# Shifting where TensorE's activations begin in SBUF, and keeping each row of 1/rms once

## The reference

```python
h = rms(x);  p = h @ w_in                        # 1024 -> 5120: q,k,v of two branches, two gates
y_a = moba(p) @ w_br_moba                        # 8 heads of 64; one block of 256: causal softmax + ALiBi
y_b = stick_breaking(p) @ w_br_sb                # 8 heads of 64; sigmoid(z) * exp(-later softplus sums)
x = x + (sigmoid(gate_a) * y_a + sigmoid(gate_b) * y_b) @ w_out
m = rms(mem)                                     # 256 memory tokens
x = x + cross_attention(rms(x) @ w_xq, m @ w_xkv) @ w_xo      # 4 heads of 128
x = x + square(relu(rms(x) @ w_up)) @ w_down     # 1024 -> 4096 -> 1024
return rms(x)
```

## Time and profile before

| | |
|---|---|
| median of 3 runs | 427.58 us |
| the profiled execution | 427.64 us, of which the span from first to last instruction is 425.5 us |
| TensorE (PE) | 413.5 us busy, 97%, 2839 matmuls |
| weight loads (PEld) | 381.0 us, 90% |
| VectorE (DVE) | 336.2 us, 79% |
| ScalarE (ACT) | 251.0 us, 59% |
| GpSimd (POOL) | 25.4 us, 6% |
| DMA | 77.47 MB, mean 182 GB/s |
| granted TensorE clock, mean | 0.995 of full speed |

### The profile page before, as it was taken

The page is one execution under the profiler, slowest core; times in us unless marked ns, Lnnn a source line. Parts: engine busy times, 40 slices in busy tenths (PEclk is TensorE's granted clock), DMA queues, the critical chain, the costliest instruction groups (busy, mean ns, idle before and its releaser), DMA issues.

```text
span 425.5 us, 7066 instructions
## 1 busy us (share of the span) xinstructions
PE 413.5 (97%) x2839; PEld 381.0 (90%) x2839; DVE 336.2 (79%) x448; ACT 251.0 (59%) x300; POOL 25.4 (6%) x39
## 2 busy tenths in 40 slices
PE   8999999999999999999999999999999999999992
PEld 7999988999999999889998899899999999999971
DVE  5588556967757536874856899999999999999956
ACT  7663238763665534551556468767777777776523
POOL 0069000000000000000200000000000000000002
PEclk9999999999999999999999999999999999999997
DMA  8999554434335255554443245465556555564002
GB/s 274 420 418 379 192 197 166 157 124 150 100 104 193 100 197 194 175 188 172 164 175 123 102 169 189 152 216 199 203 200 201 199 205 199 203 203 181 2 0 99
DMA packets 12539, 77.47 MB, mean 182 GB/s; under 512 B 1376, under 2 KB 1376, under 8 KB 4064
## 3 DMA queue, kind: packets, MB, share of 16 engines
q1 hardware_dynamic: 12512, 77.09, 50.0%
HBM read 76.04 MB, written 1.05 MB: 181 GB/s over the span
## 4 chain that ended last, share of the span: by engine, by line
PE 84%; DVE 6%; ACT 5%; issue 2%; DMA 1%; POOL 0%; POOLq 0%; SPq 0%; DVEq 0%; ACTq 0%
PE bank L1088 39%; PE bank L1354 15%; PE bank L1107 13%; PE bank L1202 10%; PE bank L1214 1%; ACT w_hi L415 1%; DVE res L1019 1%; DMA head_all<-in_head_dram 1%; DVE w_lo L662 1%; PE bank L1300 1%; DVE t_lo L662 1%; PE bank L1320 1%; DVE t_sum L914 1%; ACT mT_hi L427 1%; DVE f_lo L662 1%
## 5 line engine op out<-in xcount | busy, mean ns | idle before, releaser
L662 DVE TENSOR_TENSOR w_lo<-raw,w_hi 128x2048 fp32r<-128x2048 f32 (+2 forms) x87 | 147.4, 1702 | 26.5 <-ACT w_hi L415 25.5
L1088 PE MATMUL bank<-hT_hi,w_hi 128*128 128x256 f32 x416 | 118.4, 285 | 1.3 <-DVE w_lo L662 0.7
L1088 PE MATMUL bank<-hT_lo,w_hi 128*128 128x256 f32 x416 | 117.7, 283 | 0.0
L1088 PE MATMUL bank<-hT_hi,w_lo 128*128 128x256 f32 x416 | 117.7, 283 | 0.0
L1088 PEld LDWEIGHTS bank<-hT_hi,w_hi 128*128 128x128 f32 x416 | 79.7, 192 | 2.7 <-DVE hT_lo L712 1.1
L1088 PEld LDWEIGHTS bank<-hT_lo,w_hi 128*128 128x128 f32 x416 | 79.7, 192 | 0.6
L1088 PEld LDWEIGHTS bank<-hT_hi,w_lo 128*128 128x128 f32 x416 | 79.7, 192 | 0.0
L415 ACT ACTIVATE w_hi<-raw 128x2048 fp32r<-128x2048 f32 x33 | 62.8, 1913 | 28.2 <-PE bank L1088 15.0
L1202 PE MATMUL bank<-hT_hi,w_hi 128*128 128x256 f32 x128 | 37.1, 290 | 0.1
L662 DVE TENSOR_TENSOR t_lo<-t_sum,t_hi 128x1024 fp32r<-128x1024 f32 x30 | 36.4, 1212 | 0.0
L1202 PE MATMUL bank<-hT_lo,w_hi 128*128 128x256 f32 x128 | 36.2, 283 | 0.0
(11 more groups left out here) (195 smaller groups left out, 817.9 us busy)
## 6 DMA issues: line engine op xcount, KB each, us to landing
raw<-in_weights_dram SPq DMA_DIRECT2D x65, 1024.0 KB, 4.8
head_all<-in_head_dram SPq DMA_DIRECT2D x7, 256.0 KB, 4.8
raw<-in_chunk_dram SPq DMA_DIRECT2D x4, 256.0 KB, 5.8
raw<-in_chunk_dram SPq DMA_DIRECT2D x2, 512.0 KB, 6.9
res<-in_x_dram SPq DMA_DIRECT2D x2, 512.0 KB, 10.8
mem_tok<-in_mem_dram SPq DMA_DIRECT2D x1, 1024.0 KB, 11.5
memT_raw<-in_memT_dram SPq DMA_DIRECT2D x1, 1024.0 KB, 10.2
out_dram<-xs SPq DMA_DIRECT2D x2, 512.0 KB, 2.7
```

Of the source, the lines that this page charges most:

```text
L662: return nc.vector.tensor_tensor(dst, whole, high.bitcast(fp32), sub)
L1088: last = mm(outs[m], w, v[:, k0 + k, :], start=first and n == 0, stop=k == nk - 1 and n == 2, skip_group_check=bool(kt_wait))
```

## The change

1. `hT_hi`, `mT_hi` and `aT_hi` begin 192 bytes past a multiple of 512, `hT_lo`, `mT_lo` and `aT_lo` 320 bytes; the weights stay at 128. The high part so begins 64 bytes and the low part 192 bytes from the weights' place. `t_hi`, `f_hi`, `f_lo` and everything after them stay at 128.
2. `rstd_row` and `mem_row` hold their 256 values once; `spread` makes one copy instead of two, and the evacuations read the row twice through a broadcast pattern of [128, 2, 256]. The copies of `aT` in cross-attention take a two-block form too, since `aT` is now a slice.

```diff
+        def skip_to(place_in_512):
+            at[0] += (place_in_512 - at[0]) % 512
+        def by_tokens(name, step, place_in_512):
+            skip_to(place_in_512)
+            return place(name, [P, KT, SEQ + step // 4], f32r)
...
-        hT_hi = sb("hT_hi", [P, KT, SEQ], f32r)
-        hT_lo = sb("hT_lo", [P, KT, SEQ], f32r)
+        hT_hi_all, _ = by_tokens("hT_hi", 0, 192)
+        hT_hi = hT_hi_all[:, :, 0:SEQ]
+        hT_lo_all, _ = by_tokens("hT_lo", 0, 320)
+        hT_lo = hT_lo_all[:, :, 0:SEQ]
+        skip_to(128)
...     (mT_hi, mT_lo, aT_hi, aT_lo alike)
-        rstd_row = sb("rstd_row", [P, 2, SEQ])
-        mem_row = sb("mem_row", [P, 2, SEQ])
+        rstd_row = sb("rstd_row", [P, SEQ])
+        mem_row = sb("mem_row", [P, SEQ])
...
-                for j in range(2):
-                    last = nc.vector.tensor_copy(dst[:, j, :], bank[b][:, 0:SEQ])
-                last.then_inc(row_ready, 1)
+                nc.vector.tensor_copy(dst[:, :], bank[b][:, 0:SEQ]).then_inc(row_ready, 1)
...
-                nc.vector.tensor_tensor(flat(gateT[:, 2 * h:2 * h + 2, :]), bank[h % 2][:, :],
-                                        flat(rstd_row[:, :, :]), ALU.mult).then_inc(gate_evac, 1)
+                nc.vector.tensor_tensor(gateT[:, 2 * h:2 * h + 2, :], halves_of(bank[h % 2][:, :]),
+                                        twice(rstd_row[:, :]), ALU.mult).then_inc(gate_evac, 1)
```

More of the change, by code:

```diff
@@ L143, in hybrid_layer @@
         res = sb("res", [P, TOK, D])
-        hT_hi = sb("hT_hi", [P, KT, SEQ], f32r)
-        hT_lo = sb("hT_lo", [P, KT, SEQ], f32r)
-        mT_hi, o = place("mT_hi", [P, KT, SEQ], f32r)
+        hT_hi_all, _ = by_tokens("hT_hi", 0, 192)
[3 more added lines that the diff above has]
+        skip_to(128)
+        o = at[0]
+        mT_hi_all, _ = by_tokens("mT_hi", 0, 192)
+        mT_hi = mT_hi_all[:, :, 0:SEQ]
+        mT_lo_all, _ = by_tokens("mT_lo", 0, 320)
+        mT_lo = mT_lo_all[:, :, 0:SEQ]
+        skip_to(128)
         t_hi = sb("t_hi", [P, 2, 4 * 512], f32r, over=o)
-        mT_lo = sb("mT_lo", [P, KT, SEQ], f32r)
         qkT, o = place("qkT", [P, 16, SEQ])
@@ L166, in hybrid_layer @@
         mem_tok = sb("mem_tok", [P, TOK, D], over=o + 8192)
-        aT_hi, o = place("aT_hi", [P, 8, SEQ], f32r)
+        o = at[0]
+        aT_hi_all, _ = by_tokens("aT_hi", 0, 192)
+        aT_hi = aT_hi_all[:, :, 0:SEQ]
+        aT_lo_all, _ = by_tokens("aT_lo", 0, 320)
+        aT_lo = aT_lo_all[:, :, 0:SEQ]
+        skip_to(128)
         f_hi = sb("f_hi", [P, 2, 8 * P], f32r, over=o)
-        aT_lo, o = place("aT_lo", [P, 8, SEQ], f32r)
-        f_lo = sb("f_lo", [P, 2, 8 * P], f32r, over=o)
+        f_lo = sb("f_lo", [P, 2, 8 * P], f32r, over=o + 8192)
         alibi, o = place("alibi", [P, HEADS, SEQ])
@@ L549, in _ @@
                 act.wait_ge(x_av, 2 * p + 2)
-                copy(flat(aT_hi[:, 2 * p:2 * p + 2, :]), bank[p][:, :], ACT.Copy).then_inc(xo_hi, 1)
+                copy(aT_hi[:, 2 * p:2 * p + 2, :], bank[p].rearrange("p (b q) -> p b q", b=2), ACT.Copy)\
+                    .then_inc(xo_hi, 1)
             def arrived(c, i):
@@ L703, in spread, with halves_of, twice @@
                 dve.wait_ge(row_done, rows)
-                for j in range(2):
-                    last = nc.vector.tensor_copy(dst[:, j, :], bank[b][:, 0:SEQ])
-                last.then_inc(row_ready, 1)
+                nc.vector.tensor_copy(dst[:, :], bank[b][:, 0:SEQ]).then_inc(row_ready, 1)
+            def halves_of(t):
+                return t.rearrange("p (a n) -> p a n", a=2)
+            def twice(row):
+                return row.rearrange("p (a n) -> p a n", a=1).to_broadcast([P, 2, SEQ])
             nc.vector.memset(zeros[:, :], 0.0).then_inc(zeros_ready, 1)
@@ L730, in _ @@
                 dve.wait_ge(w_used, c + 1)
-                nc.vector.scalar_tensor_tensor(flat(qkT[:, 2 * c:2 * c + 2, :]), bank[c][:, :],
-                                               DH ** -0.5 if c % 4 < 2 else 1.0, flat(rstd_row[:, :, :]),
+                nc.vector.scalar_tensor_tensor(qkT[:, 2 * c:2 * c + 2, :], halves_of(bank[c][:, :]),
+                                               DH ** -0.5 if c % 4 < 2 else 1.0, twice(rstd_row[:, :]),
                                                ALU.mult, ALU.mult).then_inc(qk_evac, 1)
@@ L809, in mem_k_out @@
                 dve.wait_ge(w_used, MK[i] + 1)
-                nc.vector.tensor_tensor(flat(mkT[:, 2 * i:2 * i + 2, :]), bank[b][:, :], flat(mem_row[:, :, :]),
+                nc.vector.tensor_tensor(mkT[:, 2 * i:2 * i + 2, :], halves_of(bank[b][:, :]), twice(mem_row[:, :]),
                                         ALU.mult).then_inc(mk_evac, 1)
@@ L884, in _ @@
                 dve.wait_ge(xo_hi, p + 1)
-                low(flat(aT_lo[:, 2 * p:2 * p + 2, :]), bank[p][:, :], flat(aT_hi[:, 2 * p:2 * p + 2, :]))\
+                low(aT_lo[:, 2 * p:2 * p + 2, :], bank[p].rearrange("p (b q) -> p b q", b=2),
+                    aT_hi[:, 2 * p:2 * p + 2, :])\
                     .then_inc(xo_lo, 1)
```

## The result

The changed kernel takes 423.73 us (median of six executions, 423.02 to 424.03) against 427.54 (427.27 to 427.99) on the same chip: a ratio of 0.9909 [0.9896, 0.9922], 3.8 us less. The forecast was 417. The profiled execution is the shortest of the six, 423.02 us with a span of 420.9, against 427.64 and 425.5 before. Of these 4.6 us, 1.0 lies in the head, before the 216 matmuls with which the long run of query and key chunks ends. There the chain's first matmuls start at 5.19 us, and at 7.28 before, behind an input that landed earlier (at 3.57 us, and at 5.67 before). That the rest is chance is not shown.

A forecast was written before the change was run, and what follows sets the result against it. The prediction took PE's matmul spacing to bound the kernel. Copies 0.3, matmuls ahead of the MLP 7.6 and the MLP 3.0 sum to 10.9 us off 427.6, say 417, with an 8-in-10 range of 410 to 432.

The forecast's parts named there:

- What bounds the kernel: Whole kernel: PE is busy 97% of the span and holds 84% of the chain, so matmul spacing is the time.
- The copies, 0.3 us: Row copies in `spread`: one `mem_row` copy fewer on the chain saves 0.3 us; the `rstd_row` copy is covered.
- That the place matters: 256-column matmuls: stream and next weight load collide in SBUF, costing some 13 ns each; new places shorten the spacing.
- The first rival: All matmuls: the place does not matter, only the copies' 0.3 us remains, 427.3 us; chance 20%.
- I take 113, the value nearest to the 0.11 us of rows 4: 256-column matmuls: new spacing estimated at 113 ns, from the first such matmul after a 512-column one; chance 25%.
- The term of 7 ns a matmul: Ahead of the MLP: 1080 matmuls of 256 columns each save 7 ns, 7.6 us.
- the third rival: 256-column matmuls: only the high or low part escapes, mean 117 ns, half the gain, 422.2 us; chance 20%.
- The 512-column matmuls, "I take 0" of ±1.6: 512-column matmuls with moved stationary operand, 144 on the path: between 216 and 238 ns, ±1.6 us, counted as 0.
- DVE becomes the bound: MLP: PE's step falls to 10.21 us, under DVE's 10.29, so PE gains only its lag, counted as 3.0 us.
- The second (worse): 256-column matmuls: new places collide mid-stream, some 8 ns more each, 128 ns, 441.3 us; chance 20%.
- The floor of 109 ns: 256-column matmuls: collisions vanish altogether, spacing 109 ns, 412.4 us; chance 15%.
- the likeliest outcome: Whole kernel: 256-column spacing of 111 to 115 ns, giving 414 to 420 us.

The follow-up runs named there:

- e2: Changed kernel with all places as before, only the rows of 1/rms kept once: 427.19 us, ratio 0.9990.
- e1: Streams of matmuls alone, layer left out, one for each distance of moving operand from weights: 256 columns settle at 120.0 ns at 0, 113.3 at 112 and 192.
- e8: Changed kernel with high parts 112 and low parts 368 bytes from the weights' place: 419.56 us, ratio 0.9821 to the kernel before.
- e3: Changed kernel with low parts back at the weights' place, high parts still 64 bytes away: 426.25 us, ratio 0.9965.
- e4: Changed kernel with high parts back at the weights' place, low parts still 192 bytes away: 424.37 us, ratio 0.9928.
- e6: Changed kernel with high and low parts both 64 bytes from the weights' place: 424.36 us, ratio 0.9925.
- e5: Changed kernel with high and low parts both 192 bytes from the weights' place: 421.49 us, ratio 0.9870.
- e9: Streams alone, layer left out, each behind chosen other matmuls: distance 192 settles at 117.8 ns behind 512 columns, 113.3 behind 256 columns at 0 or 112.

## Why the prediction was wrong, step by step

- **What bounds the kernel: right.** PE's spacing is the time. Where it fell, the time fell.
- **The copies, 0.3 us: right.** e2 measured 0.4, and the wait for `mem_row` is gone.
- **That the place matters: right.** The first rival (20%) had it that it does not. It fell: e1 changes nothing but the distance, with no other engine writing, and goes from 120.0 to 113.3. The Trainium skill, "SBUF — State Buffer", section "Who interferes with whom", gives TensorE two independent read ports and says that PE never waits on anyone; the first rival drew from it that the places are worth nothing. For fp32r e1 differs from that by up to 6.7 ns a matmul. That stream and next weight load get in each other's way fits these runs, but what collides, and why the period is 256 bytes, no run here shows.
- **"I take 113, the value nearest to the 0.11 us of rows 4": this step failed, in size.** The term of 7 ns a matmul, 7.6 us ahead of the MLP, measured 2.2 ns. The prediction took a spacing from the first matmul after a change of shape and gave it to all. It is a real spacing of this form, but one that distance 64 does not have, and that 192 has only behind certain predecessors. Measured are 117.7, 118.6 and 117.1, nearly the third rival's 117. On the chain between the head and the MLP, against the same pieces at 120 ns, the change saves 0.48 us on the first 216, 0.63 on 336 of the gates, 0.53 on the next 240 and 0.39 on 144 of the cross-attention: 2.0 us on 936, thus 2.2 ns each and not 7. The other 144 of the 1080 lie in the head.
- **The 512-column matmuls, "I take 0" of ±1.6: in the bounds, wrong in value.** All 192 lie on PE's chain now and cost 0.22 + 0.22 + 0.25 on the three pieces of 48 and 0.17 on the rest, 0.9 us (for the second piece by the 10.91 of e2). With the copies, 0.4 + 2.0 - 0.9 is 1.5 of the 1.7 us that the trace shows ahead of the MLP.
- **In the MLP "DVE becomes the bound", 3.0: not reached, for the same reason.** At 117.1 ns a step is 10.40 and stays above 10.29; 13 steps and the last chunk give 1.85. e8, at 113 to 114, shows DVE as the bound as forecast.
- **The rivals.** The second (worse) came in the 512-column form alone. The third had the spacing and the MLP's 1.9 right, but not for its reason, so its nearness is luck: it let only one part escape, and e3 and e4 show that each part alone shortens the pieces, e6 that both at 64 come to 117.8. Its 422.2 also lacked the price of the 512 columns and counted 3.2 where 2.0 came. The floor of 109 ns was seen nowhere: 113.3 is the lowest settled value of 256 columns in any run. The measured time lies in the wide range of 410 to 432, which no change and the worse case held open, and outside the likeliest outcome's own 414 to 420.
- **A reading that does not carry what was put on it.** The prediction set fp32r against transposes and float32 products, with 109 and 216 ns, as the times of 256 and 512 columns. The trace of the kernel before lists those transposes (L1313) with 128 columns and those products (L1320) with 256, as the lines below show, so they agree with the formula only if each column is counted twice, and no run here shows that. The formula is that of the Trainium skill, "TensorE: Matmul & The Clock Gate", section "Back-to-back issue gap"; it stands there as the gap of a single matmul by itself, not of a stream of weight loads and matmuls. So these rows were no sure sign that fp32r can go faster; distance 112 in e1 is one.

```profile
L1320 PE MATMUL bank<-x_pT,mv_tok 128*128 128x256 f32 x16 | 3.6, 379 | 0.0
...
L1313 PE MATMUL bank<-ident,x_p 128*128 128x128 f32 x16 | 1.9, 272 | 0.0
```

## What to carry to other kernels

Where PE is bound by the spacing of matmuls that each load weights, the distance between the two operands' places, in 256 bytes, is a layout choice, worth up to 1.8% here. One launch of bare streams over all distances gives a first price, for every shape that uses the operand, before any tile is moved; alone it missed e5 by 4 us. So test the real order of operands and what runs before it too: a stream can have two settled spacings and keep the one into which it was led. And a spacing seen at one matmul after a change of shape shows that it is possible, not that a stream settles there.

## What had not been expected of the hardware

- The distance between moving operand and weights counts, in e1 in a period of 256 bytes: 120.0 ns at 0, 113.3 at 112 for 256 columns of fp32r. With both at 16 instead of 0 it is 118.3, which stays open.
- 512 columns have another order: lowest at 0 (226.7), up to 234.3 at 160. One layout does not serve both.
- Distance 192 has two spacings, 113.3 and 117.8, and the matmuls before decide which. It is not alone: 144 settles at 118.7 in e1 and at 116.7 in e9.
- It is a narrow thing: at 104, 108, 116 and 120 the streams of e9 settle at 120.0, 120.0, 122.5 and 120.8, around the 113.3 of 112. What in the reading of SBUF makes this pattern stays open.
